# Token one-hots built a step ahead on the vector engine, and the gate operand of a matmul laid out in pairs of tokens

## The chip, the core and the metric

The kernel runs on one core of a Trainium2 chip. Such a core has a tensor engine (PE) that multiplies matrices into banks of PSUM, a vector engine (DVE), a scalar engine (ACT), a general engine (POOL) and a queue engine (SP), which here only issues loads. They run side by side and wait for each other through semaphores. The metric is the device time of one execution in microseconds (us); less is better.

## The reference, cut to what matters

Two blocks of two layers each act on 256 tokens of 1024 features. Each layer of the first block ends in a mixture of 16384 small experts, which is where this change lies:

```python
def peer(xn, wq, k1, k2, u_tab, v_tab):
    ...
    sv, ci = lax.top_k(cand, TOPK)
    e1 = jnp.take_along_axis(i1, ci // TOPK, axis=-1)
    e2 = jnp.take_along_axis(i2, ci % TOPK, axis=-1)
    ...
    experts = (e1 * N_KEYS + e2)        # 8 heads x 16 experts for each token
    gates = jax.nn.softmax(sv, axis=-1)
    ...
    hid = jax.nn.gelu(jnp.einsum("td,tkd->tk", xi, u_tab[ei]))
    return jnp.einsum("tk,tkd->td", gi * hid, v_tab[ei])
```

Each token picks 128 experts out of 128 x 128 by two keys, e1 and e2. For each, the token's product with the expert's row of `u_tab` goes through gelu, is multiplied by a gate and weighs the expert's row of `v_tab`.

## The kernel before

**Tiles of experts.** The kernel gathers nothing. It computes all 16384 experts for all 256 tokens. A tile holds the 128 experts that share one e2; 128 "u" tiles and 128 "v" tiles of 512 KB each are read per layer, in four blocks (`EQ` = 32 tiles). The order of the blocks is written out in `PHASES`:

```python
PHASES = [("u", 0, None), ("u", 1, 0), ("v", 0, None), ("u", 2, 1), ("v", 1, None),
          ("u", 3, 2), ("v", 2, 3), ("v", 3, None)]
```

An entry is the kind of tile, the block of tiles, and the block (`qb`) whose hidden values are gated meanwhile. Four of the eight phases gate: three of kind "u", one of kind "v". A phase is a hardware loop of 4 iterations over a body of `R` = 8 steps; a step is one tile.

**A tile on PE.** Every weight is split into a high part `Wh` (ACT's cast of the loaded tile, L867, in `hi`) and the rest `Wl` (DVE's subtraction, L1232, in `lo`); the moving values are split as well. A "u" tile is 24 matmuls of 256 columns: 16 with `Wh`, 8 with `Wl` (`feature_tile`). ACT then applies gelu into `GH` (L1028) and casts the tile that is `LEAD` = 3 further on. A "v" tile is 24 such matmuls onto four banks; its moving operand is one row of `GH` over all tokens, split by ACT (L1012) and DVE (L1524) in each step. All matmuls but the transposes have the line L439 in the profile.

**The gates.** For a block of 32 keys e2, the gate matrix over (e1, token, e2) is made by matmuls. For 8 tokens per step (`BT`), DVE compares: `Aoh` is the one-hot of e1 for each token (8 instructions, L1500), `Boh` the one-hot of e2 for all 8 tokens (L1503), `Bg` is `Boh` times the gate in three bf16 parts (3 instructions, L1507). This is `spread(it, s)`. PE multiplies for each token `Aoh` (weights, 128 x 128) with the three parts of `Bg` (32 columns each): 24 matmuls per step, summed in PSUM. `gated(it, s)` on DVE (L1517) multiplies the result into `GH`. `Aoh`, `Boh`, `Bg` and the PSUM bank have two buffers each, so the one-hots of step s wait for the gate matmuls of step s-2, and the gate matmuls of step s for the gating of step s-2.

`Boh` and `Bg` lie in memory as 32 keys outside and 8 tokens inside. DVE reads and writes runs of 8; PE reads one token's 32 columns with a distance of 8 elements.

**The order on DVE** in a step s of a gated phase is: (in "v" phases the subtraction L1524 of s), `spread` of s, `lo` for the tile s+3, `gated` of s-1. On ACT in a "v" phase it is the copy L1012 of s, then the cast for s+3. On PE it is the tile s, then the gate matmuls of s. SP loads a tile when the split of the tile four before it is done (four buffers in `ring`).

Of the kernel before, what the change touches and what calls it, by code (L numbers as in the profile page):

```python
# [11 lines left out]
ALU = mybir.AluOpType  # L12
# [4 lines left out]
P = 128  # L17
# [210 lines left out]
def steps(eng, n, peel, body):  # L228

    if peel:  # L230
        body(0)
    with eng.Fori(1 if peel else 0, n) as it:
        body(it)


def build(nc, wts, mod_d, cst_d, keys_d, mla_d, bias_d, x_d, ctx_d, out_d, stop_after=None):
    ctx = ExitStack()
    with ctx:
# [95 lines left out]
        Boh = [half(BT * EQ).rearrange("p (a b) -> p a b", b=BT) for _ in range(2)]  # L334
        Bg = [half(3 * BT * EQ).rearrange("p (c a b) -> p c a b", c=3, b=BT) for _ in range(2)]
# [11 lines left out]
        iotar = half(BT * P).rearrange("p (a b) -> p a b", b=BT)  # L347
# [89 lines left out]
        def _(pe):  # L437
# [67 lines left out]
            for l in range(L):  # L505
# [115 lines left out]
                for pi, (kind, q, qb) in enumerate(PHASES):  # L621
# [9 lines left out]
                    def body(it, kind=kind, q=q, qb=qb, base=base):  # L631
                        for s in range(R):
# [16 lines left out]
                            if qb is not None:  # L649
                                n = NKEY * l + qb * EQ + s + R * it  # L650
                                pe.wait_ge(S("a_ready"), n + 1)
                                pe.wait_ge(S("b_ready"), n + 1)
                                after(pe, S("gm_ev"), n - 1)
                                for i in range(BT):
                                    for part in range(3):
                                        m = mm(bank[2 + s % 2][:, i * EQ:(i + 1) * EQ], Aoh[s % 2][:, i, :],
                                               Bg[s % 2][:, part, :, i], part == 0, part == 2)
                                m.then_inc(S("g_mm"), 1)
# [189 lines left out]
        def _(act):  # L848
# [41 lines left out]
            for l in range(L):  # L890
# [105 lines left out]
                for pi, (kind, q, qb) in enumerate(PHASES):  # L996
# [6 lines left out]
                    if kind == "v":  # L1003
                        act.wait_ge(S("gm_ev"), NKEY * l + (q + 1) * EQ)

                        def body(it, q=q, base=base):
                            for s in range(R):
                                n = NKEY * l + q * EQ + s + R * it

                                act.wait_ge(S("tile_done"), base + s - MV + 1 + R * it)  # L1010
                                act.wait_ge(S("setup"), 1)
                                nc.scalar.copy(Hh[:, s % MV, 0:T], GH[q % 2][:, bass.ds(it * R + s, 1), :]  # L1012
                                               .rearrange("p o t -> p (o t)")).then_inc(S("mv_hi"), 1)
# [3 lines left out]
                        steps(act, EQ // R, False, body)  # L1017
# [181 lines left out]
        def _(dve):  # L1199
# [78 lines left out]
            for l in range(L):  # L1278
# [204 lines left out]
                v.tensor_copy(iotar, k("iota").unsqueeze(2).broadcast_to([P, P, BT])).then_inc(S("iota_half"), 1)  # L1483
                dve.wait_ge(S("iota_half"), l + 1)
                dve.wait_ge(S("gt_ev"), 2 * (l + 1))
                for pi, (kind, q, qb) in enumerate(PHASES):
# [6 lines left out]
                    def spread(it, s, qb=qb):  # L1493
# [5 lines left out]
                        for i in range(BT):  # L1499
# [20 lines left out]
                    def body(it, kind=kind, q=q, qb=qb, base=base):  # L1520
                        for s in range(R):
                            if kind == "v":
                                dve.wait_ge(S("mv_hi"), NKEY * l + q * EQ + s + 1 + R * it)
                                v.tensor_tensor(Hl[:, s % MV, 0:T], GH[q % 2][:, bass.ds(it * R + s, 1), :]  # L1524
                                                .rearrange("p o t -> p (o t)"), Hh[:, s % MV, 0:T], ALU.subtract)\
                                    .then_inc(S("mv_lo"), 1)
# [241 lines left out]
```

## Time and profile before

| | |
|---|---|
| median of 3 runs | 4147.49 us (4143.0 to 4148.52) |
| the profiled execution | 4134.96 us, of which the span in the profile is 4133.2 us |
| granted TensorE clock, mean | 0.93 of full speed |
| busy: PE, weight loads, DVE, ACT | 88%, 80%, 61%, 34% of the span |
| the gate matmuls | 6144 of 28720 |

In a view by stretch a row gives the stretch, its length, then busy time and count of PE, PEld, DVE, ACT and POOL, the granted clock, the DMA share and GB/s. In the profile PE is the matmul side of TensorE and PEld its weight loads, which overlap the matmuls. "Idle before" is the time an engine stood still ahead of an instruction, with what released it. The granted clock is a share of 2.4 GHz and has two levels, 1.0 and 0.5 (1.2 GHz). Matmuls are pipelined, so recorded ones overlap; the distance between the starts of two groups is what a group costs.

### The profile page before, as it was taken

The page shows a single profiled execution, that of the slowest core. Times are in us where ns is not written, and L with a number is a line of the kernel's source. Part 1 is how long each engine was busy: PE and PEld are TensorE (multiplying, and loading weights), DVE is VectorE, ACT ScalarE, POOL GpSimd, SP SyncE. Part 2 cuts the span into 40 slices and gives each one's busy share as a digit, 9 for nine tenths or more (in the row PEclk, how much of TensorE's full clock was granted, in tenths as well). Part 3 has the DMA queues.
Part 4 walks back from the last instruction along what each step waited for, and adds up shares of the span by engine and source line. Part 5 has one row for each costly group of instructions (what it writes and reads, how often), then busy time and mean ns, then how long its engine had stood idle before and what let it go on. Part 6 is the DMA issues. An engine that isn't in the chain of part 4 may idle for free.

```text
span 4133.2 us, 77923 instructions
## 1 busy us (share of the span) xinstructions
PE 3633.6 (88%) x28720; PEld 3289.2 (80%) x28720; DVE 2505.4 (61%) x6350; ACT 1392.3 (34%) x2128; POOL 331.0 (8%) x216
## 2 busy tenths in 40 slices
PE   7779789899899887978998999988785999799898
PEld 6579789889899765978998989976554887587698
DVE  6359765766796553987566578746465223464544
ACT  3234224233233433332322423343242223332443
POOL 1237000000000012730000000000000000000000
PEclk9689899999999977989999999999897999899999
DMA  6534325334334554442433433331101222121153
GB/s 236 171 103 153 103 97 168 102 129 141 102 119 141 175 172 135 142 142 97 145 125 106 164 105 115 123 131 61 36 1 41 87 97 97 67 92 49 54 180 132
DMA packets 131691, 478.51 MB, mean 116 GB/s; under 512 B 14512, under 2 KB 16560, under 8 KB 130992
## 3 DMA queue, kind: packets, MB, share of 16 engines
q1 hardware_dynamic: 115696, 416.72, 30.0%
q0 software_dynamic: 15808, 59.25, 4.3%
q8 instruction: 122, 2.00, 0.2%
q14 instruction: 65, 0.53, 0.0%
HBM read 474.87 MB, written 1.05 MB: 115 GB/s over the span
## 4 chain that ended last, share of the span: by engine, by line
PE 72%; DVE 18%; issue 4%; ACT 3%; DMA 2%; DVEq 1%; POOL 0%; ACTq 0%; SPq 0%
PE bank L439 71%; DVE arena L1500 2%; ACT Wh L867 2%; DMA HA<-mods 1%; DVE Wl L1232 1%; DVE arena L1414 1%; DVE arena L1580 1%; DVE arena L1411 1%; DVE arena L1435 1%; DVE arena L1410 1%; DVE arena L1413 1%; DVE arena L1412 1%; PE bank L681 1%; DVE arena L1456 1%; DVE arena L1453 1%
## 5 line engine op out<-in xcount | busy, mean ns | idle before, releaser
L439 PE MATMUL bank<-HR,Wh 128*128 128x256 f32 (+1 forms) x12288 | 1864.7, 306 | 156.9 <-DVE HR L1575 60.0
L439 PEld LDWEIGHTS bank<-HR,Wh 128*128 128x128 f32 x12288 | 1681.1, 198 | 243.9 <-issue 77.2
L1232 DVE TENSOR_TENSOR Wl<-ring,Wh 128x1024 fp32r<-128x1024 f32 x692 | 847.3, 1225 | 1172.8 <-ACT Wh L867 1165.8
L867 ACT CAST Wh<-ring 128x1024 fp32r<-128x1024 f32 x788 | 823.5, 1045 | 836.9 <-PE bank L439 833.7
L439 PE MATMUL bank<-HR,Wl 128*128 128x256 f32 (+1 forms) x6144 | 951.8, 298 | 13.8 <-DVE Wl L1232 7.5
L439 PEld LDWEIGHTS bank<-HR,Wl 128*128 128x128 f32 x6144 | 848.1, 194 | 44.8 <-DVE Wl L1232 7.9
L439 PE MATMUL bank<-arena 128*128 128x32 bf16 (+4 forms) x6624 | 560.3, 256 | 135.9 <-issue 76.0
L439 PEld LDWEIGHTS bank<-arena 128*128 128x128 bf16 (+3 forms) x6624 | 442.0, 123 | 206.5 <-issue 151.8
L1028 ACT ACTIVATE arena<-bank 128x256 f32 x256 | 98.5, 385 | 788.8 <-PE bank L439 788.6
L1500 DVE TENSOR_SCALAR arena<-arena 128x128 bf16<-128x128 bf16 x2048 | 355.6, 251 | 0.1
L1726 POOL TENSOR_TENSOR Wl<-ring,Wh 128x1024 fp32r<-128x1024 f32 x96 | 247.5, 2591 | 146.2 <-ACT Wh L867 145.9
L439 PE MATMUL bank<-arena,K 128*128 128x256 f32 (+2 forms) x322 | 134.8, 565 | 93.8 <-ACT arena L854 53.9
L1507 DVE TENSOR_TENSOR arena<-arena 128x256 bf16<-128x256 bf16 x768 | 178.1, 287 | 29.6
L439 PEld LDWEIGHTS bank<-arena,K 128*128 128x128 f32 (+1 forms) x322 | 69.0, 226 | 141.9 <-issue 50.8
L1737 POOL DMA_DIRECT2D HA<-mods x96 | 72.1, 754 | 1286.4 <-PE bank L439 1272.8
L439 PE MATMUL bank<-Wh,HR 128*128 128x128 f32 x1024 | 174.5, 278 | 0.0
L439 PEld LDWEIGHTS bank<-Wh,HR 128*128 128x128 f32 x1024 | 155.9, 192 | 4.2 <-issue 4.2
L1580 DVE RECIPROCAL arena<-arena 128x512 f32<-128x512 f32 (+1 forms) x39 | 117.7, 3019 | 39.2 <-ACT arena L1051 39.2
L439 PE MATMUL bank<-Wl,HR 128*128 128x128 f32 x512 | 140.9, 275 | 0.0
L1524 DVE TENSOR_TENSOR HR<-arena,HR 128x256 fp32r<-128x256 f32 x256 | 107.4, 419 | 7.0 <-ACT HR L1012 7.0
L1012 ACT CAST HR<-arena 128x256 fp32r x256 | 102.9, 402 | 24.5 <-DVE arena L1517 24.5
L1517 DVE TENSOR_TENSOR arena<-arena,bank 128x256 f32 (+1 forms) x256 | 105.7, 415 | 6.3 <-PE bank L439 6.3
(222 smaller groups left out, 1938.9 us busy)
## 6 DMA issues: line engine op xcount, KB each, us to landing
ring<-weights SPq DMA_DIRECT2D x788, 512.0 KB, 3.3
HA<-mods POOLq DMA_DIRECT2D x96, 512.0 KB, 6.0
arena<-bias POOLq DMA_DIRECT2D x16, 256.0 KB, 2.9
arena<-keys POOLq DMA_DIRECT2D x2, 1024.0 KB, 5.6
HA<-mla POOLq DMA_DIRECT2D x1, 1536.0 KB, 6.7
K<-constants SPq DMA_DIRECT2D x1, 1402.0 KB, 5.8
X<-x SPq DMA_DIRECT2D x1, 1024.0 KB, 8.4
X<-context POOLq DMA_DIRECT2D x1, 1024.0 KB, 7.2
```

The costliest lines, as they stand in the source:

```text
L439: return nc.tensor.matmul(out, lhsT, rhs, start=first, stop=last)
L867: nc.scalar.copy(Wh[:, i % SPL], ring[:, i % RAW]).then_inc(S("hi_done"), 1)
L1012: nc.scalar.copy(Hh[:, s % MV, 0:T], GH[q % 2][:, bass.ds(it * R + s, 1), :] .rearrange("p o t -> p (o t)")).then_inc(S("mv_hi"), 1)
L1028: nc.scalar.activation(o, bank[s % 2][:, 0:T], ACT.Gelu_apprx_tanh).then_inc(S("h_ev"), 1)
L1232: v.tensor_tensor(Wl[:, i % SPL], ring[:, i % RAW], Wh[:, i % SPL], ALU.subtract).then_inc(S("lo_done"), 1)
L1500: m = v.tensor_scalar(Aoh[s % 2][:, i, :], iotah, i1c[:, bass.ds(it * (R * BT) + s * BT + i, 1)], None, ALU.is_equal)
L1507: m = v.tensor_tensor(Bg[s % 2][:, part], Boh[s % 2], gpart[:, part, at].unsqueeze(1).broadcast_to([P, EQ, BT]), ALU.mult)
L1517: v.tensor_tensor(g, g, bank[2 + s % 2][:, 0:BT * EQ].rearrange("p (t e) -> p e t", t=BT), ALU.mult).then_inc(S("gm_ev"), 1)
L1524: v.tensor_tensor(Hl[:, s % MV, 0:T], GH[q % 2][:, bass.ds(it * R + s, 1), :] .rearrange("p o t -> p (o t)"), Hh[:, s % MV, 0:T], ALU.subt ...
L1580: seq(v.reciprocal(grs[j % 2][:, 0:width], grt[j % 2][:, 0:width]))
L1726: nc.gpsimd.tensor_tensor(Wl[:, i % SPL], ring[:, i % RAW], Wh[:, i % SPL], ALU.subtract)\
L1737: pool.dma_start(mslot[n % MSLOT], mod_d[n].rearrange("p (a b) -> p a b", a=4)).then_inc(S(f"mod_in{n % MSLOT}"), 16)
```

## The change

It has three parts.

1. On DVE, `spread` runs a step ahead. The first is made before the loop; then a step is `gated` of s-1, `spread` of s+1, `lo` for s+3. The last iteration of the loop is written out (`tail`), so that it can leave out what would run past the end.
2. In "v" phases, ACT's copy and DVE's subtraction of the hidden values run two steps ahead (`h_high`, `h_low`), with two of each before the loop.
3. `Boh` and `Bg` are laid out as 4 pairs of tokens outside, 32 keys, and the 2 tokens of a pair inside. PE reads a token's columns with a distance of 2 elements. DVE's operands follow: `pairs(...)` reads two tokens, repeats them for 32 keys and goes to the next pair. The constant `iotar` shrinks to two copies of each key.

```diff
-def steps(eng, n, peel, body):
+def steps(eng, n, peel, body, tail=False):
     if peel:
         body(0)
-    with eng.Fori(1 if peel else 0, n) as it:
+    with eng.Fori(1 if peel else 0, n - 1 if tail else n) as it:
         body(it)
+    if tail:
+        body(n - 1)
+
+def last(it):
+    return isinstance(it, int) and it == EQ // R - 1
...
-        Boh = [half(BT * EQ).rearrange("p (a b) -> p a b", b=BT) for _ in range(2)]
-        Bg = [half(3 * BT * EQ).rearrange("p (c a b) -> p c a b", c=3, b=BT) for _ in range(2)]
+        Boh = [half(BT * EQ).rearrange("p (a b c) -> p a b c", b=EQ, c=2) for _ in range(2)]
+        Bg = [half(3 * BT * EQ).rearrange("p (d a b c) -> p d a b c", d=3, b=EQ, c=2) for _ in range(2)]
...
-                                               Bg[s % 2][:, part, :, i], part == 0, part == 2)
+                                               Bg[s % 2][:, part, i // 2, :, i % 2], part == 0, part == 2)
...
+                        def h_high(s, it, q=q, base=base):
+                            act.wait_ge(S("tile_done"), base + s - MV + 1 + R * it)
+                            act.wait_ge(S("setup"), 1)
+                            nc.scalar.copy(Hh[:, s % MV, 0:T], GH[q % 2][:, bass.ds(it * R + s, 1), :]
+                                           .rearrange("p o t -> p (o t)")).then_inc(S("mv_hi"), 1)
...
                             for s in range(R):
+                                if s + 2 < R or not last(it):
+                                    h_high(s + 2, it)
                                 hi_next[0] = base + s + LEAD
                                 hi(base + s + LEAD, it)
-                        steps(act, EQ // R, False, body)
+                        for s in range(2):
+                            h_high(s, 0)
+                        steps(act, EQ // R, False, body, True)
...
-                v.tensor_copy(iotar, k("iota").unsqueeze(2).broadcast_to([P, P, BT])).then_inc(S("iota_half"), 1)
+                v.tensor_copy(iotar, k("iota").unsqueeze(2).broadcast_to([P, P, 2])).then_inc(S("iota_half"), 1)
...
-                        v.tensor_tensor(Boh[s % 2], if12h[:, 1, at].unsqueeze(1).broadcast_to([P, EQ, BT]),
-                                        iotar[:, qb * EQ:(qb + 1) * EQ, :], ALU.is_equal).then_inc(S("b_hot"), 1)
+                        def pairs(a):
+                            return a.rearrange("p (a c) -> p a c", c=2).unsqueeze(2).broadcast_to([P, BT // 2, EQ, 2])
+
+                        v.tensor_tensor(Boh[s % 2], pairs(if12h[:, 1, at]),
+                                        iotar[:, qb * EQ:(qb + 1) * EQ, :].unsqueeze(1).broadcast_to([P, BT // 2, EQ, 2]),
+                                        ALU.is_equal).then_inc(S("b_hot"), 1)
                         dve.wait_ge(S("b_hot"), n + 1)
                         for part in range(3):
                             m = v.tensor_tensor(Bg[s % 2][:, part], Boh[s % 2],
-                                                gpart[:, part, at].unsqueeze(1).broadcast_to([P, EQ, BT]), ALU.mult)
+                                                pairs(gpart[:, part, at]), ALU.mult)
...
                         for s in range(R):
+                            ahead = s + 1 < R or not last(it)
+                            if kind == "v" and (s + 2 < R or not last(it)):
+                                h_low(s + 2, it)
                             if qb is not None:
-                                spread(it, s)
+                                if s or not isinstance(it, int) or it:
+                                    gated(it, s - 1)
+                                if ahead:
+                                    spread(it, s + 1)
                             lo_next[0] = base + s + LEAD
                             lo(base + s + LEAD, it)
-                            if qb is not None and (s or not isinstance(it, int) or it):
-                                gated(it, s - 1)
-                    steps(dve, EQ // R, qb is not None, body)
+                    if kind == "v":
+                        for s in range(2):
+                            h_low(s, 0)
+                    if qb is not None:
+                        spread(0, 0)
+                    steps(dve, EQ // R, qb is not None, body, True)
```

## Rows read from the trace of the kernel before

**Rows 1.** The page: busy time by engine (share, count), and the load of a tile.
```profile
PE 3633.6 (88%) x28720; PEld 3289.2 (80%) x28720; DVE 2505.4 (61%) x6350; ACT 1392.3 (34%) x2128; POOL 331.0 (8%) x216
...
ring<-weights SPq DMA_DIRECT2D x788, 512.0 KB, 3.3
```

**Rows 2.** Busy time by stretch, gated "u" phases: one and the sum of six.
```profile
446.70:621.40 174.70, 152.13 (x1536) 147.90 (x1536) 120.50 (x450) 47.33 (x68) 0.00 (x0) 0.93 0.28 94
...
sum 997.50, PE 882.06 PEld 855.09 DVE 712.38 ACT 263.39 POOL 0.00; mean PE 147.01 PEld 142.52 DVE 118.73 ACT 43.90 POOL 0.00
```

**Rows 3.** The same view of the two gated "v" phases: their sum.
```profile
sum 284.54, PE 283.62 PEld 280.51 DVE 261.13 ACT 84.79 POOL 0.00; mean PE 141.81 PEld 140.25 DVE 130.56 ACT 42.39 POOL 0.00
```

**Rows 4.** Timeline of a gated "v" step: start us, us, engine, line, operation.
```profile
1231.30 1.60 PE L439 MATMUL bank<-arena 128*128 128x32 bf16 x24
...
1231.75 0.70 DVE L1507 TENSOR_TENSOR arena<-arena 128x256 bf16<-128x256 bf16 x3
...
1232.58 1.22 DVE L1232 TENSOR_TENSOR Wl<-ring,Wh 128x1024 fp32r<-128x1024 f32 x1
1232.67 2.00 PEld L439 LDWEIGHTS bank<-HR,Wh 128*128 128x128 f32 x16
...
1235.67 1.42 PEld L439 LDWEIGHTS bank<-arena 128*128 128x128 bf16 x24
```

**Rows 5.** Timeline of a gated "u" step.
```profile
804.12 1.11 PE L439 MATMUL bank<-HR,Wl 128*128 128x256 f32 x8
...
805.64 1.04 ACT L867 CAST Wh<-ring 128x1024 fp32r<-128x1024 f32 x1
...
806.71 1.23 DVE L1232 TENSOR_TENSOR Wl<-ring,Wh 128x1024 fp32r<-128x1024 f32 x1 [3.06 <-ACT Wh L867]
807.85 0.41 DVE L1517 TENSOR_TENSOR arena<-arena,bank 128x256 f32 x1
808.18 1.39 DVE L1500 TENSOR_SCALAR arena<-arena 128x128 bf16<-128x128 bf16 x8
...
809.91 0.69 DVE L1507 TENSOR_TENSOR arena<-arena 128x256 bf16<-128x256 bf16 x3
...
810.87 1.60 PE L439 MATMUL bank<-arena 128*128 128x32 bf16 x24 [1.28 <-DVE arena L1507]
```

**Rows 6.** Timeline around the start of a loop iteration.
```profile
494.12 1.28 ACT L1028 ACT_TABLE_LOAD   x1 [4.20 <-PE bank L439]
...
496.76 1.23 DVE L1232 TENSOR_TENSOR Wl<-ring,Wh 128x1024 fp32r<-128x1024 f32 x1 [2.92 <-ACT Wh L867]
...
499.97 0.69 DVE L1507 TENSOR_TENSOR arena<-arena 128x256 bf16<-128x256 bf16 x3
500.58 1.22 DVE L1232 TENSOR_TENSOR Wl<-ring,Wh 128x1024 fp32r<-128x1024 f32 x1
```

**Rows 7.** Busy time by stretch inside gate groups; the last, of PE alone, opens one.
```profile
1827.20:1827.90 0.70, 0.70 (x14) 0.70 (x14) 0.00 (x0) 0.43 (x1) 0.00 (x0) 0.50 0.00 0
1828.00:1828.45 0.45, 0.45 (x12) 0.45 (x10) 0.00 (x0) 0.45 (x1) 0.00 (x0) 1.00 0.00 0
...
810.86:810.92 0.06, 0.05 (x2) 1.00 0.21 69
```

**Rows 8.** Timeline: a tile at 1.2 GHz and the gates behind it.
```profile
446.73 3.78 PE L439 MATMUL bank<-HR,Wh 128*128 128x256 f32 x16 [3.23 <-DVE arena L1481]
...
452.02 1.64 PE L439 MATMUL bank<-arena 128*128 128x32 bf16 x24
```

**Rows 9.** Groups by line and shape: count, busy us, mean ns of one, idle before.
```profile
L439 PEld LDWEIGHTS bank<-HR,Wh 128*128 128x128 f32 x12288 | 1681.1, 198 | 243.9 <-issue 77.2 <-DVE HR L1575 62.8 <-DVE HR L1524 17.1
...
L439 PEld LDWEIGHTS bank<-arena 128*128 128x128 bf16 x6144 | 367.5, 116 | 140.3 <-issue 112.6 <-DVE arena L1500 20.9
...
L1507 DVE TENSOR_TENSOR arena<-arena 128x256 bf16<-128x256 bf16 x768 | 178.1, 287 | 29.6
...
L1524 DVE TENSOR_TENSOR HR<-arena,HR 128x256 fp32r<-128x256 f32 x256 | 107.4, 419 | 7.0 <-ACT HR L1012 7.0
```

More of the change, by code:

```diff
@@ L346, in build @@
         iotah = half(P)
-        iotar = half(BT * P).rearrange("p (a b) -> p a b", b=BT)
+        iotar = half(2 * P).rearrange("p (a b) -> p a b", b=2)
         i12u, ciu = i12.bitcast(U32), ci.bitcast(U32)
@@ L1004, in _, with body @@
                         act.wait_ge(S("gm_ev"), NKEY * l + (q + 1) * EQ)
-                        def body(it, q=q, base=base):
-                            for s in range(R):
[L1008 to L1013, printed above, removed]
+                        def h_high(s, it, q=q, base=base):
[3 more added lines that the diff above has]
+                                           .rearrange("p o t -> p (o t)")).then_inc(S("mv_hi"), 1)
+                        def body(it, base=base):
+                            for s in range(R):
+                                if s + 2 < R or not last(it):
+                                    h_high(s + 2, it)
                                 hi_next[0] = base + s + LEAD
                                 hi(base + s + LEAD, it)
-                        steps(act, EQ // R, False, body)
+                        for s in range(2):
+                            h_high(s, 0)
+                        steps(act, EQ // R, False, body, True)
                         hi_next[0] = base + EQ + LEAD
@@ L1518, in gated, with h_low, body @@
                                         ALU.mult).then_inc(S("gm_ev"), 1)
-                    def body(it, kind=kind, q=q, qb=qb, base=base):
-                        for s in range(R):
[L1522 to L1526, printed above, removed]
+                    def h_low(s, it, q=q):
+                        dve.wait_ge(S("mv_hi"), NKEY * l + q * EQ + s + 1 + R * it)
+                        v.tensor_tensor(Hl[:, s % MV, 0:T], GH[q % 2][:, bass.ds(it * R + s, 1), :]
+                                        .rearrange("p o t -> p (o t)"), Hh[:, s % MV, 0:T], ALU.subtract)\
+                            .then_inc(S("mv_lo"), 1)
+                    def body(it, kind=kind, qb=qb, base=base):
+                        for s in range(R):
+                            ahead = s + 1 < R or not last(it)
+                            if kind == "v" and (s + 2 < R or not last(it)):
+                                h_low(s + 2, it)
                             if qb is not None:
-                                spread(it, s)
+                                if s or not isinstance(it, int) or it:
+                                    gated(it, s - 1)
+                                if ahead:
+                                    spread(it, s + 1)
                             lo_next[0] = base + s + LEAD
                             lo(base + s + LEAD, it)
-                            if qb is not None and (s or not isinstance(it, int) or it):
-                                gated(it, s - 1)
-                    steps(dve, EQ // R, qb is not None, body)
+                    if kind == "v":
[4 more added lines that the diff above has]
+                    steps(dve, EQ // R, qb is not None, body, True)
                     if qb is not None:
```

## The prediction

> **What bounds the kernel now.** I read the busy times first. TensorE (PE) is busy 88% of the span, VectorE (DVE) 61% [rows 1]. That is an average over stages of different kinds, so the next view is busy time by stretch, one stretch per phase that the change touches. In the six gated "u" phases (a "u" tile and the gate matmuls of an earlier block in each step) 997.5 us pass with PE at 882.1 busy and DVE at 712.4 [rows 2]: PE has holes and nobody else is full. In the two gated "v" phases PE is busy for 283.6 of 284.5 us, DVE for 261.1 [rows 3]. The same matmuls thus take much longer in one kind of phase than in the other, and the timelines say why.
>
> In a gated "v" step [rows 4] gate matmuls start at 1231.30, the next tile at 1232.67, the next gates at 1235.67: 1.37 us for 24 gate pairs (weight load and matmul, 57 ns each), 3.00 us for the tile's 24 pairs (125 ns each), 4.37 us in all and no hole. In a gated "u" step [rows 5] PE stands still 1.28 us before the gates at 810.87, until DVE's L1507 (the gated one-hots) is done. Back from there: the one-hots begin at 808.18, behind the gating at 807.85, behind the split of tile weights L1232 at 806.71, and that waited for ACT's cast at 805.64, which with the gelu ahead of it waited for the end of PE's tile at 805.23. So one-hots that need nothing from this tile queue behind a split that does. From tile end 805.23 to one-hots ready at 810.6 are 5.4 us; PE needs gates and next tile, 4.37. The step after it is free of the wait, because PE's lateness gave DVE time: long and short steps alternate. At the start of a loop iteration ACT also loads a table for 1.28 us (494.12), which comes on top of the same chain: the split follows only at 496.76 [rows 6].
>
> **Part 1: one-hots a step ahead.** DVE's order was: one-hots of s, split for s+3, gating of s-1. It becomes gating of s-1, one-hots of s+1, split for s+3. Nothing is removed: it is one rotation of the same cycle. One-hots of s+1 now need only the gates of s-1, whose buffers they reuse, and are asked for a tile, a gate group and a tile later (3.00+1.37+3.00 = 7.4 us); the gating and the one-hots take 807.85 to 810.6, 2.8 us [rows 5]. The wait goes whole, table load too, since 4.6 us are to spare.
>
> What is late next: the split, by the 2.8 us now ahead of it. It waits for the same cast at about 1.45 us behind the tile's end, by which time the one-hots (begun when the gates of the step before ended, 3.00 us before the tile's end) are just over: so the split hardly moves. PE asks for its result three tiles on. Behind the split on DVE stand the gating of s and the one-hots of s+2, ready at 1.45+3.8 = 5.3 us behind the tile's end and asked for at 2 x 4.37 = 8.7 us. SP's load of a tile waits for the split of four tiles before; it lands 3.3 us after issue in the median [rows 1] and has over two steps. The buffers' own rule (gates of s wait for the gating of s-2) is met a step early. So the cost of the move is nothing while the step is over about 4 us.
>
> Worth: with steps of 4.37 us the phases that are counted from their first gates would take 31 x 4.37 + 1.4 = 136.8 us; the two that are counted from their first tile 142.1, that tile running cold (5.3 us in each). 4 x 136.8 + 2 x 142.1 = 831.4 against 997.5 [rows 2]: 166 us. I take off 4 for cold remnants: **162 us**. The clock there is 0.93 of full in the first phase [rows 2]; part of the gain is its rise, and the step of 4.37 us, which is one at full clock, has it in it.
>
> **Part 2: the "v" hidden halves two steps ahead.** ACT's copy and DVE's subtraction for s+2 instead of s. PE already has no hole in these phases [rows 3], so 0. At each phase's start two copies instead of one go ahead; the first releases the first subtraction as before, so the hand-over between phases stays. ACT's cast then stands behind one more copy of about 0.4 us, once, covered by three tiles already split.
>
> **Part 3: the layout.** Boh and Bg become pairs of tokens inside, 32 keys, four pairs outside. On PE the columns of a gate matmul lie 2 elements apart instead of 8; on DVE four instructions per step read and write innermost runs of 2 instead of 8.
>
> *PE's side.* A gate pair costs 57 ns for 32 columns, a tile pair 125 for 256. At the tile's rate 32 columns are 16 ns. What holds the gates? Two rows speak against the array clock: with 0.50 granted (1.2 GHz) 0.70 us hold 14 gate matmuls, with 1.00 (2.4 GHz) 0.45 us hold 12, those in flight counted; pairs at twice 57 ns would leave 6 starts in the first [rows 7]. A tile pair nearly doubles: the tile at 446.73 took 5.3 us, one at full clock 3.00 [rows 4, 8]. The weight load of the gates is recorded as 116 ns against 198 for f32 [rows 9], so it is the shorter part. A cost of reading columns 16 bytes apart fits all of this. New price: between 16 ns (below it nothing speaks) and 57. The two matmuls that open a group at 810.86 both start within 0.06 us [rows 7], before any steady rate holds them; I take 38 ns. PE's step is then 4.37 - 24 x 0.019 = 3.91 us.
>
> The Trainium skill ("SBUF — State Buffer", Door 1: The DMA port swizzle, in the note on cachelines) has SBUF lines of 16 bytes, of which at least two hits each are wanted for full rate. By it the old operand hits each line once and the new one four times, and the sum would be the one below; no row here shows lines as such.
>
> *DVE's side.* The four instructions are 128x256 in bf16 and take 0.287 us, read off L1507, which is three of them [rows 9]. The innermost run is still contiguous and even, all operands are bf16: I price them as unchanged. Bounds: 0 and the f32 price for the same 256 elements, 0.419 [rows 9], that is +0.53 us a step.
>
> *Who sets the step now.* DVE with no wait: split at 496.76, next split at 500.58, 3.82 us [rows 6]. PE would need 3.91, at the lower bound 3.4. So DVE is a floor just below: I take 3.90 for "u". In "v" DVE has the subtraction as well; its cycle of 4.37 holds a hole of 0.13 us before the split at 1232.58, where without a wait L1507 overlaps the next by 0.08 [rows 4, 6]: 0.21 to gain, floor 4.16, taken as 4.18. Worth: 186 "u" steps (31 in each of six phases) x 0.47 = **88 us**, 62 "v" steps x 0.19 = **12 us**. A much faster gate pair would give only 186 x 0.08 = 15 us more, as DVE then binds.
>
> The constant iotar shrinks to a quarter, twice a kernel: less than one split's 1.23 us [rows 6], 0 in the sum. The last loop iteration is written out, which needs more code; no row shows code loading held against these phases, 0.
>
> **Sum.** 162 + 88 + 12 = 262 us. The profiled execution took 4135.0 us (span 4133.2): 4135 - 262 = 3873. The runs' median is 12 us above that execution; I put the forecast between, at **3880**.
>
> **Rivals.**
> A. *The gates keep their price* (22%). 57 ns at both clock levels is also what a fixed cost of handing a pair to the array looks like, and I have no gate matmul with close columns. Then parts 1 and 2 only: 4135 - 162 = 3973. For it: the flatness; against it: the shorter opening pair. The Trainium skill ("TensorE: Matmul & The Clock Gate", Wait — 56ns, not 53.3ns?) names 62 ns per matmul as a floor with hardware decode off, and by that page nothing would be gained from closer columns, which gives this rival's time; no row here shows which decode is on.
> B. *DVE falls to the one-element rate on runs of two* (7%). +0.53 us a step: "u" 4.35, "v" 4.69. 162 + 186 x 0.02 - 62 x 0.32 = 146: 3989.
> C. *A new wait eats part of the rotation* (4%), such as ACT's table load reaching DVE now that DVE is nearly full: 1.28 us per 8 steps, 186/8 x 1.28 = 30 us less than forecast: about 3905.
> D. *Slower* (3%). The same mechanism as B, but with a cost for each run of two. DVE's step would have to grow by x with 186 x (5.25 - 3.82 - x) + 62 x (0.21 - x) = 0, so x = 1.13 us (5.25 is the mean step now, 4.37 + 166/186), the instructions at 0.57 us instead of 0.287. Twice the f32 row, 0.84 us each, gives x = 2.2 and +268 us: about 4400. Below 0.57 us each the change wins.
> E. *No change* (1%): the holes come from something else that is late at the same time. Against it: the chain of [rows 5] has no other wait of that size.
>
> **Numbers.** The forecast has 63% with a range of its own of 3850 to 3915: below, DVE's floors of 3.82 and 4.16 throughout; above, C. The range for all takes in rival A and runs from 3840 to 3985, leaving out B, D and E. A measurement of this kernel cannot tell 0.2% (8 us) from nothing; every case but D and E is far beyond it: faster 0.95, same 0.02, slower 0.03.
>
> **What would show it.** Part 1: in the gated "u" phases no wait of PE for the gated one-hots, steps nearly even, clock near 0.99. Part 3: gate groups of about 0.9 us instead of 1.37, at either clock level; the Boh and Bg instructions still near 0.287. Together: "u" phases of about 122 us and "v" gated ones near 134, with DVE about 95% busy in both. Wrong would be gate groups of 1.37 (A), DVE instructions above 0.4 (B), DVE idle before its split while PE waits (C).

## The result and the profile after

| | before | after |
|---|---|---|
| median of 4 runs each, us | 4145.27 (4143.0 to 4148.52) | 3828.73 (3827.23 to 3833.27) |
| profiled execution: span, us | 4133.2 | 3831.4 |
| granted clock, mean | 0.932 | 0.933 |

The ratio is 0.9238, with a 95% interval of 0.9222 to 0.9254. The change takes 317 us from the median and 302 from the span. The profiled execution of before lay 10 us under its median, that of after 5 above (3833.3). On the profile's scale, on which the prediction's sum was made, the sum gave 3873 and the measurement is 3833, 40 us faster. The median lies 11 us below the range's lower end of 3840.

In the new program the matmul line L439 is L446, the one-hots of e1 L1500 are L1512, `Boh` is L1518, `Bg` L1523 (was L1507), the gating L1533 (was L1517), the split L1244 (was L1232), the subtraction of hidden values L1539 (was L1524).

The page after, busy by engine, against [rows 1]:

```profile
PE 3405.4 (89%) x28720; PEld 3057.1 (80%) x28720; DVE 2484.3 (65%) x6350; ACT 1391.4 (36%) x2128; POOL 330.9 (9%) x216
```

The counts are the same, so no work went away. PE's busy time fell by 228 us all the same: most of that is gate groups, which are recorded with 0.75 to 0.77 us instead of 1.60 (409.3 us in sum before, 194.2 after), the rest is mainly matmuls that ran at 1.2 GHz before.

The rest is easiest to see if the span is cut at the gates, from the first gate matmul of a gated phase to the last. The columns are those of [rows 2]. Before, as three answers: the sum of the eight gated stretches, of the six that lie between two of them, and of everything else:

```profile
sum 1255.00, PE 1143.43 PEld 1115.02 DVE 952.48 ACT 346.77 POOL 0.00; mean PE 142.93 PEld 139.38 DVE 119.06 ACT 43.35 POOL 0.00
...
sum 416.80, PE 404.74 PEld 399.64 DVE 225.12 ACT 176.91 POOL 0.00; mean PE 67.46 PEld 66.61 DVE 37.52 ACT 29.49 POOL 0.00
...
sum 2461.40, PE 2085.44 PEld 1774.52 DVE 1327.80 ACT 868.60 POOL 330.95; mean PE 695.15 PEld 591.51 DVE 442.60 ACT 289.53 POOL 110.32
```

The same after; of the gated stretches a "u" and a "v" one are shown too:

```profile
673.80:789.00 115.20, 114.22 (x1513) 110.34 (x1512) 112.02 (x428) 41.37 (x64) 0.00 (x0) 1.00 0.42 137
...
1013.40:1136.40 123.00, 115.05 (x1513) 110.53 (x1512) 120.24 (x450) 41.06 (x59) 0.00 (x0) 1.00 0.39 129
...
sum 941.00, PE 917.38 PEld 883.15 DVE 910.38 ACT 340.60 POOL 0.00; mean PE 114.67 PEld 110.39 DVE 113.80 ACT 42.58 POOL 0.00
...
sum 417.70, PE 397.62 PEld 396.73 DVE 238.63 ACT 183.17 POOL 0.00; mean PE 66.27 PEld 66.12 DVE 39.77 ACT 30.53 POOL 0.00
...
sum 2472.70, PE 2090.44 PEld 1777.21 DVE 1335.32 ACT 867.63 POOL 330.92; mean PE 696.81 PEld 592.40 DVE 445.11 ACT 289.21 POOL 110.31
```

The gated stretches lost 314.0 us (1255.0 to 941.0), those between grew by 0.9, all other stages by 11.3: 302 won in sum. So everything was won where the change is. DVE is now as full as PE (910 against 917 of 941), and both have idle time, in different steps.

How such steps look is in PE's timeline. Near the start of the first gated phase the steps are even and short:

```profile
460.87 0.77 PE L446 MATMUL bank<-arena 128*128 128x32 bf16 x24
461.49 2.16 PE L446 MATMUL bank<-HR,Wh 128*128 128x256 f32 x16
...
464.45 0.77 PE L446 MATMUL bank<-arena 128*128 128x32 bf16 x24
```

From gates to the next gates it is 464.45 - 460.87 = 3.58 us (3.57 in most pairs), from gates to the tile behind them 0.62 us. That is 26 ns a pair for 24 pairs, where the same two starts lay 1.41 apart at a distance of 8 (59 ns; shown below). Some 60 us on, the splits of DVE lie 3.81 us apart, and so do PE's gates:

```profile
520.38 1.22 DVE L1244 TENSOR_TENSOR Wl<-ring,Wh 128x1024 fp32r<-128x1024 f32 x1
...
524.19 1.22 DVE L1244 TENSOR_TENSOR Wl<-ring,Wh 128x1024 fp32r<-128x1024 f32 x1
...
524.38 0.75 PE L446 MATMUL bank<-arena 128*128 128x32 bf16 x24
...
528.19 0.75 PE L446 MATMUL bank<-arena 128*128 128x32 bf16 x24
```

### The profile page after: what moved, and what is told of

Its sections match the earlier page's. It is cut to its first block, busy times and chain, and to the rows that moved or that the text cites. A ratio compares the mean times of both kernels' runs of the same rounds, so it can differ in the third digit from the quotient of the medians.

```text
span 3831.4 us, 76570 instructions
## 1 busy us (share of the span) xinstructions
PE 3405.4 (89%) x28720; PEld 3057.1 (80%) x28720; DVE 2484.3 (65%) x6350; ACT 1391.4 (36%) x2128; POOL 330.9 (9%) x216
## 4 chain that ended last, share of the span: by engine, by line
PE 71%; DVE 21%; issue 3%; ACT 2%; DMA 2%; DVEq 1%; POOL 0%; SPq 0%; ACTq 0%
PE bank L446 70%; DVE arena L1512 2%; DVE Wl L1244 2%; DMA HA<-mods 1%; DVE arena L1426 1%; DVE arena L1606 1%; DVE arena L1423 1%; DVE arena L1447 1%; DVE arena L1422 1%; DVE arena L1425 1%; DVE arena L1424 1%; PE bank L688 1%; DVE arena L1523 1%; DVE arena L1468 1%; ACT Wh L874 1%
## 5 line engine op out<-in xcount | busy, mean ns | idle before, releaser
L446 PE MATMUL bank<-HR,Wh 128*128 128x256 f32 (+1 forms) x12288 | 1831.3, 303 | 167.2 <-DVE HR L1601 60.0
L446 PEld LDWEIGHTS bank<-HR,Wh 128*128 128x128 f32 x12288 | 1654.3, 195 | 250.2 <-issue 77.3
L1244 DVE TENSOR_TENSOR Wl<-ring,Wh 128x1024 fp32r<-128x1024 f32 x692 | 845.7, 1223 | 897.4 <-ACT Wh L874 895.9
L446 PE MATMUL bank<-HR,Wl 128*128 128x256 f32 (+1 forms) x6144 | 950.0, 298 | 13.8 <-DVE Wl L1244 7.5
L446 PEld LDWEIGHTS bank<-HR,Wl 128*128 128x128 f32 x6144 | 844.8, 193 | 44.8 <-DVE Wl L1244 7.9
L446 PE MATMUL bank<-arena 128*128 128x32 bf16 (+4 forms) x6624 | 346.2, 199 | 47.9 <-issue 13.5
L1512 DVE TENSOR_SCALAR arena<-arena 128x128 bf16<-128x128 bf16 x2048 | 355.3, 249 | 0.1
L446 PEld LDWEIGHTS bank<-arena 128*128 128x128 bf16 (+3 forms) x6624 | 247.4, 104 | 123.3 <-issue 90.2
L446 PE MATMUL bank<-arena,K 128*128 128x256 f32 (+2 forms) x322 | 137.6, 575 | 93.8 <-ACT arena L861 54.0
L1523 DVE TENSOR_TENSOR arena<-arena 128x256 bf16<-128x256 bf16 x768 | 178.4, 287 | 23.6 <-DVE arena L1518 0.8
L446 PEld LDWEIGHTS bank<-arena,K 128*128 128x128 f32 (+1 forms) x322 | 70.0, 229 | 143.3 <-issue 52.3
L446 PE MATMUL bank<-Wh,HR 128*128 128x128 f32 x1024 | 174.5, 278 | 0.0
L446 PEld LDWEIGHTS bank<-Wh,HR 128*128 128x128 f32 x1024 | 156.1, 192 | 4.2 <-issue 4.2
L446 PE MATMUL bank<-Wl,HR 128*128 128x128 f32 x512 | 140.9, 275 | 0.0
L1539 DVE TENSOR_TENSOR HR<-arena,HR 128x256 fp32r<-128x256 f32 x256 | 106.4, 419 | 4.3 <-ACT HR L1017 4.3
L1017 ACT CAST HR<-arena 128x256 fp32r (+1 forms) x256 | 101.3, 402 | 21.2 <-DVE arena L1533 21.2
L1533 DVE TENSOR_TENSOR arena<-arena,bank 128x256 f32<-128x256 f32 (+1 forms) x256 | 106.1, 414 | 0.0
```

The source lines that it names most:

```text
L446: return nc.tensor.matmul(out, lhsT, rhs, start=first, stop=last)
L1244: v.tensor_tensor(Wl[:, i % SPL], ring[:, i % RAW], Wh[:, i % SPL], ALU.subtract).then_inc(S("lo_done"), 1)
L1512: m = v.tensor_scalar(Aoh[s % 2][:, i, :], iotah, i1c[:, bass.ds(it * (R * BT) + s * BT + i, 1)], None, ALU.is_equal)
L1523: m = v.tensor_tensor(Bg[s % 2][:, part], Boh[s % 2], pairs(gpart[:, part, at]), ALU.mult)
L1533: v.tensor_tensor(g, g, bank[2 + s % 2][:, 0:BT * EQ].rearrange("p (t e) -> p e t", t=BT), ALU.mult).then_inc(S("gm_ev"), 1)
```

## The experiments

Four questions: what each part is worth alone, what price the gate pair has by distance, whether DVE's floor is what holds the step now, and what the phases' hand-over costs. The runs of before beside them had medians of 4148.45, 4146.58 and 4146.70 us (7, 7 and 9 runs).

### Parts 1 and 2 without the layout: order_only

The changed kernel with 8 tokens inside, as before:

```diff
-    ... rearrange("p (a b c) -> p a b c", b=EQ, c=2)   # Boh; Bg likewise
+    ... rearrange("p (a b c) -> p a b c", b=EQ, c=8)
...
-    Bg[s % 2][:, part, i // 2, :, i % 2]
+    Bg[s % 2][:, part, i // 8, :, i % 8]
```

`iotar` and `pairs` follow with 8 in place of 2.

> Parts 1 and 2 of the change with the old layout (a token's columns 8 elements apart). Theory: the column distance alone sets the price of a gate pair. Then gate groups stay at 1.37 us, gated u steps go to an even 4.37 us, gated v steps stay at 4.37 us, and the time is about 3985 us beside 4145 before (162 us less). Rival: the gates became cheap because nothing waits in front of them any more. Then groups drop to about 0.6 us here too and the time is near 3830 us.

Measured: 3974.24 us, ratio 0.9581 (0.9565 to 0.9597). PE's timeline in a gated "u" phase:

```profile
951.42 1.60 PE L446 MATMUL bank<-arena 128*128 128x32 bf16 x24
952.83 2.16 PE L446 MATMUL bank<-HR,Wh 128*128 128x256 f32 x16
...
955.79 1.60 PE L446 MATMUL bank<-arena 128*128 128x32 bf16 x24
```

Every step has 4.37 us (955.79 - 951.42), 1.41 of it for the gates. The chain of [rows 5] is gone, and the profiled execution, 3973.1 us, is where the prediction's 4135 - 162 puts it. The gated stretches of this kernel have 1093.8 us in sum, 161.2 less than before, and all of it comes from the "u" ones: each "v" one has 136.7 us, as before. So part 2, which is in this kernel too, gives nothing in a gated "v" phase at the old price of the gates, and the 161 us are part 1's. The rotation is read rightly, the table load included.

### Part 3 without the order: layout_only

The kernel before, with the diff's lines for `Boh`, `Bg`, `iotar` and `pairs`, and nothing else of it:

```diff
-        Boh = [half(BT * EQ).rearrange("p (a b) -> p a b", b=BT) for _ in range(2)]
+        Boh = [half(BT * EQ).rearrange("p (a b c) -> p a b c", b=EQ, c=2) for _ in range(2)]
...
-                                               Bg[s % 2][:, part, :, i], part == 0, part == 2)
+                                               Bg[s % 2][:, part, i // 2, :, i % 2], part == 0, part == 2)
```

> Part 3 alone, in the old order. Theory: gate groups 0.6 us; in gated u phases the one-hots are still late behind the split, so steps alternate between about 5.4 and 3.8 us, mean near 4.6 (5.25 before), and gated v steps fall to DVE's 4.15 us; about 4010 us. Rival: in the u phases PE waits for DVE anyway, so cheaper gates give nothing there and only the v phases gain: about 4130 us.

Measured: 4109.09 us, 0.9912 (0.9896 to 0.9929), 39 us. My figure of 4010 was far off. A gated "u" stretch of this kernel, by busy time, and PE's timeline in it:

```profile
717.20:875.80 158.60, 128.84 (x1512) 124.50 (x1511) 115.65 (x434) 42.15 (x64) 0.00 (x0) 0.89 0.31 103
```
```profile
740.73 0.75 PE L439 MATMUL bank<-arena 128*128 128x32 bf16 x24 [1.63 <-issue]
741.33 3.19 PE L439 MATMUL bank<-HR,Wh 128*128 128x256 f32 x16
...
745.79 0.77 PE L439 MATMUL bank<-arena 128*128 128x32 bf16 x24
...
803.62 0.82 PE L439 MATMUL bank<-arena 128*128 128x32 bf16 x24 [2.04 <-DVE arena L1511]
```

The gates are cheap here too (0.60 us). But in the old order they stand behind the chain through ACT and DVE, and that is as long as ever: PE waits 1.63 us ahead of the first group shown, and 2.04 us ahead of the one at 803.62, where the record names DVE's products (L1511 in this kernel). PE idles more, the granted clock is 0.87 to 0.90 in the "u" stretches (0.95 to 0.99 before), and the tile at 741.33 lasts 4.46 us instead of 2.96. So most of the 0.8 us per step turns into waiting, and a part of what is left is lost to the clock. By stretch, the six "u" ones give 18 us (981.6 to 963.6) and the two "v" ones, where PE had no hole before, 20 (273.4 to 252.9). Parts 1 and 2 without the layout give 174 us and the layout alone 39, 213 together; the change gives 317. The order is what makes the layout pay.

### No hidden halves ahead: no_hidden_ahead

The changed kernel, with the hidden halves of s made in step s, as before, and none ahead of the loop:

```diff
-                                if s + 2 < R or not last(it):
-                                    h_high(s + 2, it)
+                                h_high(s, it)
...
-                            if kind == "v" and (s + 2 < R or not last(it)):
-                                h_low(s + 2, it)
+                            if kind == "v":
+                                h_low(s, it)
```

> The changed kernel without part 2: the hidden values of v tiles are split in their own step again. Theory: part 2 is worth nothing, same time as the changed kernel, 3829 us within 5. Rival: with steps of 3.6 to 4.15 us the halves come late when they are made in their own step, gated v steps go back above 4.3 us and the time is 20 us or more above.

Measured: 3854.96 us, 0.9289 (0.9274 to 0.9305): 26 us slower than the change. In an ungated "v" phase of this kernel, then of after, PE's timeline:

```profile
860.30 2.08 PE L446 MATMUL bank<-HR,Wh 128*128 128x256 f32 x16
...
863.20 2.17 PE L446 MATMUL bank<-HR,Wh 128*128 128x256 f32 x16
...
866.16 2.08 PE L446 MATMUL bank<-HR,Wh 128*128 128x256 f32 x16
```
```profile
863.10 2.08 PE L446 MATMUL bank<-HR,Wh 128*128 128x256 f32 x16
...
865.98 2.08 PE L446 MATMUL bank<-HR,Wh 128*128 128x256 f32 x16
```

Without part 2 two tiles in turn take 2.90 and 2.96 us (860.30, 863.20, 866.16); with it each takes 2.88 (865.98 - 863.10). The profile shows no idle time for either, because recorded matmuls overlap (2.08 us recorded, the next group 1.92 later): a hole of a tenth of a microsecond vanishes in the record. By the sums of the two traces, part 2 is worth 13.1 us in the stretches between the gated ones (430.8 against 417.7 us) and 9.4 in the gated ones (950.4 against 941.0; all of it in the "v" ones, 127.4 and 128.0 against 123.0). In a gated "v" step of this kernel PE does wait in the record, for DVE's subtraction (L1536 here):

```profile
1058.23 2.18 PE L446 MATMUL bank<-HR,Wh 128*128 128x256 f32 x16 [0.40 <-DVE HR L1536]
```

With the old price of the gates there was no such wait: the "v" stretches have 136.7 us in before and in order_only alike. Cheaper gates made it.

### The price of a gate pair by distance: distance_4, distance_1, distance_16

distance_4 and distance_1 are the changed kernel with c=4 and c=1 in place of c=2 (first pair of lines below); distance_16 keeps `Boh` at c=8 and writes the products into the first 8 of every 16 places of a `Bg` twice as long (the last pair below, which PE reads with i // 8 and i % 8):

```diff
-                                               Bg[s % 2][:, part, i // 2, :, i % 2], part == 0, part == 2)
+                                               Bg[s % 2][:, part, i // 4, :, i % 4], part == 0, part == 2)
...
+        Bg = [half(3 * 16 * EQ).rearrange("p (d a b c) -> p d a b c", d=3, b=EQ, c=16) for _ in range(2)]
...
+                            m = v.tensor_tensor(Bg[s % 2][:, part, :, :, 0:BT], Boh[s % 2],
```

> The changed kernel with four tokens inside instead of two: columns 4 elements (8 bytes) apart. Theory of a threshold: the price is flat up to some distance, groups stay at 0.58 us and the time at 3829 us. Rival, a price that grows with the distance (25 ns at 2, 57 at 8): about 36 ns at 4, groups 0.86 us, PE step 3.85 instead of 3.57, about 3855 us.

> The changed kernel with a token's columns side by side (distance 1 element), eight tokens outside. Theory for PE: at distance 2 something else than the moving operand holds the pair at 25 ns, so it stays there; rival: the price falls again, below 22 ns. For DVE the token's value is now an operand repeated 32 times in the innermost run; theory: the four instructions fall to the one-element rate, 0.42 us as in f32, DVE's cycle is 4.35 us in u and 4.68 in v, and the time is 3829 + 186 x 0.6 + 62 x 0.7 = about 3985 us; rival: they stay at 0.287 and the time at 3829.

> The order of the changed kernel, the old layout for the one-hot of e2, and its three products laid with a gap of 8 unused elements behind each 8, so that PE's columns lie 16 elements (32 bytes) apart. Theory: from 8 elements on every column is fetched on its own, so the price stays at 57 to 59 ns a pair and the time at 3974 us. Rival: the price keeps growing with the distance, about 110 ns at 16, steps of 5.6 us, and the time is near 4280 us.

PE's timelines of distance_4, distance_1 and distance_16, in this order:

```profile
902.05 0.91 PE L446 MATMUL bank<-arena 128*128 128x32 bf16 x24
902.80 2.15 PE L446 MATMUL bank<-HR,Wh 128*128 128x256 f32 x16
```
```profile
723.42 0.76 PE L446 MATMUL bank<-arena 128*128 128x32 bf16 x24 [0.62 <-DVE arena L1523]
724.03 2.15 PE L446 MATMUL bank<-HR,Wh 128*128 128x256 f32 x16
```
```profile
721.91 1.60 PE L446 MATMUL bank<-arena 128*128 128x32 bf16 x24
723.31 2.16 PE L446 MATMUL bank<-HR,Wh 128*128 128x256 f32 x16
```

| distance, elements (bytes) | gates to tile, us | ns a pair | median, us | ratio (95%) |
|---|---|---|---|---|
| 1 (2) | 0.61 | 25 | 3963.63 | 0.9565 (0.9549 to 0.9581) |
| 2 (4), the change | 0.62 | 26 | 3828.73 | 0.9238 (0.9222 to 0.9254) |
| 4 (8) | 0.75 | 31 | 3836.24 | 0.9241 (0.9223 to 0.9258) |
| 8 (16), order_only | 1.41 | 59 | 3974.24 | 0.9581 (0.9565 to 0.9597) |
| 16 (32) | 1.40 | 58 | 3970.30 | 0.9574 (0.9558 to 0.9590) |

Nothing in PE's instructions differs between these kernels but the distance of the columns, and the price follows it: rival A is refuted. Going from 2 to 1 gives nothing more, and going from 8 to 16 costs nothing more. Both theories for distance 4 missed: the price there, 31 ns, is neither that of distance 2 nor the 36 of a straight line. The Trainium skill ("TensorE: Matmul & The Clock Gate", Back-to-back issue gap) has an issue floor of about 25 ns for matmuls of 1 to 64 columns. The trace agrees with 25 to 26 ns at distances 1 and 2. The Trainium skill's floor of 62 ns with hardware decode off (the same page, Wait — 56ns, not 53.3ns?), named beside rival A, does not hold here: 26 ns lie far below it, and so did the 57 ns of [rows 4]. The Trainium skill's rule on two hits per 16-byte line ("SBUF — State Buffer", Door 1: The DMA port swizzle, the note on cachelines) agrees in the large: one hit per line costs 59 ns, and two (distance 4) 31. But two are not yet free, four are.

Distance 1 also shows what it costs on DVE. The group of `Bg` by form, and DVE's timeline:

```profile
L1523 DVE TENSOR_TENSOR arena<-arena 128x256 bf16<-128x256 bf16 x768 | 280.8, 421 | 23.2 <-DVE arena L1518 0.8
```
```profile
723.10 1.22 DVE L1244 TENSOR_TENSOR Wl<-ring,Wh 128x1024 fp32r<-128x1024 f32 x1
...
727.44 1.22 DVE L1244 TENSOR_TENSOR Wl<-ring,Wh 128x1024 fp32r<-128x1024 f32 x1
```

With the keys innermost, one operand repeats a single element, and an instruction takes 421 ns, the f32 price of [rows 9]. The cycle is 4.34 us (727.44 - 723.10), PE's step with it, and the kernel takes 3963.63 us (3985 expected). This is rival B's mechanism, at the price that the prediction gave it, in a layout with runs of one. In the Trainium skill ("Vector Engine (DVE) Microarchitecture Reference", section 5.1 on performance modes) the mode that packs two 16-bit values asks for a step of one in every operand, and the trace agrees. In runs of two the rate stays, as this row of after shows:

```profile
L1523 DVE TENSOR_TENSOR arena<-arena 128x256 bf16<-128x256 bf16 x768 | 178.4, 287 | 23.6 <-DVE arena L1518 0.8 <-issue 0.4
```

### DVE's floor: one_a, one_ab, one_a_distance_4

If DVE holds the step, less work on DVE must move it. one_a lays `Aoh` out in pairs as well and builds it with one instruction instead of eight; the weights are then read 2 elements apart:

```diff
-                        for i in range(BT):
-                            m = v.tensor_scalar(Aoh[s % 2][:, i, :], iotah, i1c[...], None, ALU.is_equal)
-                        m.then_inc(S("a_ready"), 1)
+                        v.tensor_tensor(Aoh[s % 2], pairs(if12h[:, 0, at], P),
+                                        iotar[:, :, :].unsqueeze(1).broadcast_to([P, BT // 2, P, 2]),
+                                        ALU.is_equal).then_inc(S("a_ready"), 1)
```

one_ab does the three products of `Bg` in one instruction too. one_a_distance_4 is one_a with `Boh` and `Bg` at distance 4.

> The changed kernel, but DVE makes the eight one-hots of e1 in one instruction of 128x1024 in bf16, in the same pairs layout, instead of eight of 128x128; PE reads its weights with columns 2 elements apart. Theory: DVE's cycle (3.81 us in gated u steps, 4.15 in v) is what holds the steps above PE's 3.57; the one instruction takes about 0.6 us from start to start instead of 1.30, DVE's cycle falls to about 3.1 and 3.45, every gated step goes to 3.57, and the time is 3829 - 186 x 0.15 - 62 x 0.38 = 3778 us. Rival: weight loads with distant columns cost PE more, at worst the 57 ns per pair of the old moving operand, and the time goes back to about 3974 us.

> As the kernel with one instruction for the one-hots of e1, and the three products with the gate's parts in one instruction of 128x768 too. Theory: PE holds the step by then, so nothing more is gained: the same time within 5 us, about 3778 us. Rival: DVE still delays something (the splits of weights or hidden values), then 10 us or more are gained over the other.

> The kernel with one instruction for the one-hots of e1 and with the products of e2 at distance 4 instead of 2. Theory: distance 4 costs PE 0.13 us more a step (3.70 for 3.57), which did not show in the time while DVE held the step; now it does: 3774 + 248 x 0.13 = 3806 us. Rival: the dearer gates stay hidden, 3774 us.

Measured: one_a 3773.67 us, 0.9105 (0.9090 to 0.9120); one_ab 3772.13, 0.9096 (0.9080 to 0.9110); one_a_distance_4 3815.21, 0.9197 (0.9181 to 0.9213). The sum over the gated stretches of one_a, by busy time, its groups by form, and its timelines of PE and DVE:

```profile
sum 892.90, PE 892.86 PEld 880.23 DVE 764.93 ACT 339.97 POOL 0.00; mean PE 111.61 PEld 110.03 DVE 95.62 ACT 42.50 POOL 0.00
```
```profile
L1514 DVE TENSOR_TENSOR arena<-arena 128x1024 bf16<-128x1024 bf16 x256 | 175.4, 685 | 0.1
L446 PEld LDWEIGHTS bank<-arena 128*128 128x128 bf16 x6144 | 171.0, 97 | 11.1
```
```profile
903.35 0.77 PE L446 MATMUL bank<-arena 128*128 128x32 bf16 x24
903.97 2.15 PE L446 MATMUL bank<-HR,Wh 128*128 128x256 f32 x16
...
905.01 1.23 DVE L1244 TENSOR_TENSOR Wl<-ring,Wh 128x1024 fp32r<-128x1024 f32 x1 [0.37 <-ACT Wh L874]
...
906.92 0.77 PE L446 MATMUL bank<-arena 128*128 128x32 bf16 x24
```

One instruction of 0.69 us replaces eight that take 1.39 together. PE is now busy for 892.86 of 892.90 us at 3.57 a step, and DVE waits 0.37 us before its split. So DVE held the step in after: 48 us in the gated stretches (941.0 to 892.9), 55 in the median. one_ab shortens DVE further (one product of 128x768 in 0.56 us for three that take 0.69) and gives nothing, as it must once DVE has time to spare. And distance 4, which cost no measurable time while DVE held the step (0.9241 against 0.9238), costs some 40 us here. Its gates start at 901.02 and 904.76, 3.74 us apart, against 3.57 in one_a: 248 steps by 0.17 are 42 us, and the medians differ by 41.5.

### The hand-over between phases: one_a_handover

one_a, with the last gating put ahead of the last split of a phase:

```diff
                                 if ahead:
                                     spread(it, s + 1)
+                                else:
+                                    gated(it, s)
...
-                    if qb is not None:
-                        gated(EQ // R - 1, R - 1)
```

> The kernel with one instruction for the one-hots of e1, and in the last step of a gated phase DVE does the last gating before the split of the tile three on, not behind it. Theory: from the last gate matmul of a u phase to the first matmul of the v phase pass 3.4 to 3.6 us (2.25 before the change) because the last gating waits behind that split; with the swap six of these hand-overs lose about 1.3 us each, 3774 - 8 = 3766 us. Rival: the split is then late for PE, which gives the same back: 3774 us.

After a gated phase the "v" tiles need its last gating. Timelines around the end of the first gated phase, of after and of one_a_handover:

```profile
573.14 0.75 PE L446 MATMUL bank<-arena 128*128 128x32 bf16 x24
...
574.65 1.22 DVE L1244 TENSOR_TENSOR Wl<-ring,Wh 128x1024 fp32r<-128x1024 f32 x1
575.79 0.41 DVE L1533 TENSOR_TENSOR arena<-arena,bank 128x256 f32<-128x256 f32 x1
...
577.16 0.45 PE L446 MATMUL bank<-HR,Wh 128*128 128x256 f32 x1 [3.27 <-DVE HR L1539]
```
```profile
564.65 0.42 DVE L1533 TENSOR_TENSOR arena<-arena,bank 128x256 f32<-128x256 f32 x1 [1.16 <-PE bank L446]
...
567.12 1.58 PE L446 MATMUL bank<-HR,Wh 128*128 128x256 f32 x11 [2.50 <-DVE HR L1539]
```

In after the gates end at about 573.9 and the gating, which could start then, stands behind a split until 575.79; PE is idle for 3.27 us, against 2.01 before:

```profile
622.89 3.45 PE L439 MATMUL bank<-HR,Wh 128*128 128x256 f32 x15 [2.01 <-DVE HR L1524]
```

That is the row of before. With the gating ahead of the split PE waits 2.49 or 2.50 us in each of the six places, where one_a has 3.38 to 3.46, and the stretches between the gated ones fall from 417.0 us in one_a to 406.7. The waits are 5.5 us of that. The rest goes along with the granted clock: it is 1.00 in two of the four long stretches and 0.98 in the others, and 0.98 in all four in one_a. The median is 3768.06 us, 0.9094 (0.9080 to 0.9107). This cannot be told from one_a (0.9105, 0.9090 to 0.9120); the ten microseconds are seen in the trace alone. It is the version with the lowest median.

## Why the prediction was too high

**Part 1, 162 us.** Right, by order_only: 3973.1 against 3973 on the profile's scale, and 161.2 us in the gated stretches. No wait for the one-hots is left and the clock in the gated stretches is 1.00.

**A price taken too high: "I take 38 ns" for a gate pair.** It is 26 ns; the bounds of 16 and 57 held it. PE's step is 2.96 + 0.62 = 3.57 us where the prediction has 3.91. The opening pair of [rows 7] had spoken for a number far under 57; I went to the middle of the bounds without a row that asked for it, and no row of before could give the number. By itself this is the smaller part of the miss: with 26 ns and the prediction's own floors, "u" steps of 3.82 and "v" steps of 4.16 us, the sum would have been 16 us lower, 3857, still inside the range.

**The step that failed: "A much faster gate pair would give only 186 x 0.08 = 15 us more, as DVE then binds."** The floor of 3.82 is real (3.81 in the timeline of after), but it is not a floor for a phase, for two reasons. First, PE enters a phase with a stock, since one-hots are a step and splits three tiles ahead, and runs at 3.57 us until it is used up: five to twelve steps in the "u" phases, nine in the "v" ones. Second, 3.82 was read in a step of the hardware loop. In the iterations that are written out, the first and the last, DVE's own cycle is shorter; here are two splits of the first one:

```profile
460.18 1.23 DVE L1244 TENSOR_TENSOR Wl<-ring,Wh 128x1024 fp32r<-128x1024 f32 x1 [3.38 <-ACT Wh L874]
...
463.88 1.22 DVE L1244 TENSOR_TENSOR Wl<-ring,Wh 128x1024 fp32r<-128x1024 f32 x1
```

They lie 3.70 us apart, and nothing waits between them. In the last iteration DVE has the same 3.70, and PE's gates with it (4.04 in "v" instead of 4.15). The 0.11 us lie between `Boh` and the first `Bg`: L1523 starts 0.43 us behind L1518 in a looped step (519.34 to 519.77), 0.32 in the step shown (462.95 to 463.27). Without the last group of 0.58 us each, the six "u" stretches (695.0 us in sum) give (695.0 - 3.5) / 186 = 3.72 us a step, not 3.90: 34 us. The two "v" ones give (246.0 - 1.2) / 62 = 3.95, not 4.18: 14 us. Of these 48 us 16 are the price of the pair, as above, and 32 the floors. Why the gap is shorter without the loop was not tested. That the stock makes the short steps is read from the trace, and it fits one_a, where DVE is never late and nearly every step has 3.57.

**The last gate group of a phase.** Left in the sum at its old price: eight times 0.78 us, 6 us.

**"PE already has no hole in these phases [rows 3], so 0" (part 2).** Wrong in size: part 2 is worth 26 us within the changed kernel. For the gated "v" phases the reading was right as long as the gates kept their price, for order_only has the same 136.7 us; it stopped being right with part 3, which the sum didn't carry over to part 2. And the part also works in the "v" phases without gates, which the prediction never priced; there the holes of 0.1 us can't be seen in a busy share, because recorded matmuls overlap.

**"So the hand-over between phases stays."** It did not. In the new order the last split starts at 574.65, when the last gates have ended, and the last gating waits behind it. The wait of PE grew from 2.01 to 3.27 us in the place shown. What part 2 gives between the gated stretches and what the hand-over takes nearly cancel: 416.8 to 417.7 us. Two zeros of the sum were two terms of about ten.

**The sum.** 34 + 14 + 6 = 54 faster than predicted by the terms above. By the stretches' sums it is 314.0 - 262 = 52. Less 0.9 between and 11.3 elsewhere, 40 are left, the distance of 3873 to 3833. (186 x 0.47 is 87.4, where the prediction has 88.) The 11.3 us lie in stages that the change does not touch. The same sum is 2460.2 us in one_a (3770.1 - 892.9 - 417.0), 2464.1 in order_only, 2471.6 in layout_only and 2476.0 in no_hidden_ahead (3857.2 - 950.4 - 430.8), with 2461.4 before. It does not follow the change, so 11 us are within what differs from one execution to the next; nine runs of before spread from 4136.1 to 4151.6 us. What moves it stays open.

**The rivals.** A is refuted by the table of distances; its time, 3973, is that of order_only. B's mechanism exists at runs of one; at runs of two the row stays 287 ns. C did not come: a table load of 1.28 us stands at 516.93 in after, and the splits go on at 3.81 us beside it (516.57 to 520.38):

```profile
516.57 1.22 DVE L1244 TENSOR_TENSOR Wl<-ring,Wh 128x1024 fp32r<-128x1024 f32 x1
...
516.93 1.28 ACT L1040 ACT_TABLE_LOAD   x1 [2.61 <-PE bank L446]
```

Nothing of D or E showed. As for the signs named ahead: "u" phases of about 122 us came out at 115.2 to 116.8 from first gate to last (122.0 with the cold tile ahead of the first), "v" gated ones near 134 at 123.0, gate groups of 0.9 at 0.62. DVE was 95 to 98% busy, as named.

## What to carry to other kernels

For short matmuls look early at the distance of the moving operand's columns: with 32 bf16 columns, 2 elements apart instead of 8 took a weight load and matmul from 59 to 26 ns, while runs of two kept DVE's rate. A floor from another engine bounds the steady step, not a phase that starts with a stock, and it holds for the form of the loop in which it was read (3.81 us looped, 3.70 written out). When two engines are within a few per cent, work out both (here 3.57 and 3.81 us) and keep both for the range. And a cheaper operation pays only when nothing late stands ahead of it: layout and order gave 39 and 174 us apart, 317 together. It also makes new waits: part 2 was worth nothing in the gated "v" phases until the gates were cheap, 9 us then.

## What was not expected of the hardware

- The price of 32 bf16 columns has three levels: 25 to 26 ns a pair at 2 or 4 bytes apart, 31 at 8 (0.78 us for the group, 33 ns, in one_a_distance_4, where the weights lie 2 elements apart too), 58 to 59 at 16 and 32. It hardly follows the clock. The first gates of after start at 457.21, the tile behind them at 457.91, 0.70 us for 24 pairs with 0.51 granted (1.2 GHz), against 0.62 at full clock. The stretch around them, by busy time:

```profile
456.80:457.90 1.10, 1.10 (x27) 1.01 (x27) 0.00 (x0) 0.37 (x1) 0.00 (x0) 0.51 0.00 0
```

- Weights 2 elements apart cost next to nothing: 97 ns a load in one_a, 96 in after, with 0.62 us for the group in both.
- A one-hot by comparison of two bf16 tensors of 1024 elements takes 0.685 us. Eight comparisons of 128 with a value per partition take 1.39.
